# Computing gelu(x U) of three token tiles as dense products and gathering values from a prepared table

## What is computed

```python
def peer(h, w_q, keys, u_tab, v_tab):        # for each block xb of 128 tokens
    q = einsum('td,de->te', xb, w_q).reshape(128, 8, 2, 128)
    s = einsum('thpd,hpkd->thpk', q, keys)                    # scores, two axes of 128 keys
    s_top, i_top = lax.top_k(s, 16)                           # 16 best on each axis
    cand = s_top[:, :, 0, :, None] + s_top[:, :, 1, None, :]  # 256 candidates
    best, sel = lax.top_k(cand, 16)                           # 16 experts a head: eidx
    gate = jax.nn.softmax(best, axis=-1)
    act = jax.nn.gelu(einsum('td,thkd->thk', xb, u_tab[eidx]), approximate=False)
    return einsum('thk,thkd->td', gate * act, v_tab[eidx])
```

## Time and profile before

| | |
|---|---|
| median of 3 runs | 2221.38 us (2214.74 to 2225.39) |
| the profiled execution: span | 2217.6 us |
| busy: TensorE, VectorE, ScalarE, GpSimd | 1812.9, 1313.7, 872.2, 632.8 us |
| moved by DMA | 637 MB, 545 of it by the gathers |
| first gather issued, first dot | 852.6, 859.0 us |
| two ScalarE steps of a slot (L2077, L2082) | 0.20 and 0.29 us |

### The profile page before, as it was taken

The page is one execution under the profiler, slowest core; times in us unless marked ns, Lnnn a source line. Parts: engine busy times, 40 slices in busy tenths (PEclk is TensorE's granted clock), DMA queues, the critical chain, the costliest instruction groups (busy, mean ns, idle before and its releaser), DMA issues.

```text
span 2217.6 us, 25834 instructions
## 1 busy us (share of the span) xinstructions
PE 1812.9 (82%) x8648; PEld 1169.7 (53%) x8648; DVE 1313.7 (59%) x2828; ACT 872.2 (39%) x2271; POOL 632.8 (29%) x553
## 2 busy tenths in 40 slices
PE   5989889979987888898887777777777777777776
PEld 4988889969966887565532222222323322222222
DVE  3127353353363537677766766767667866766764
ACT  4223322242244324444434444444443444444443
POOL 0002012100000002454434444444344443444442
PEclk8999899979998998999999999999999999999999
DMA  3313122335015329999999999999999999999997
GB/s 115 123 44 94 29 58 72 99 104 180 22 65 192 115 76 367 334 413 416 395 393 419 420 419 420 420 420 418 393 420 409 419 418 419 402 420 420 419 415 301
DMA packets 171933, 637.36 MB, mean 287 GB/s; under 512 B 12546, under 2 KB 97605, under 8 KB 104856
## 3 DMA queue, kind: packets, MB, share of 16 engines
q0 software_dynamic: 74880, 545.29, 60.0%
q1 hardware_dynamic: 96928, 90.50, 12.9%
HBM read 617.92 MB, written 17.93 MB: 287 GB/s over the span
## 4 chain that ended last, share of the span: by engine, by line
DMA 31%; PE 13%; DVE 8%; ACT 8%; issue 3%; DVEq 0%; ACTq 0%
DMA ex_uv_row<-in_peer_uv,ex_eidx 31%; PE ps L1995 10%; DVE ex_uv_row L2228 5%; ACT ex_spread L2087 2%; ACT L2077 1%; ACT ret_tables L2082 1%; ACT L2071 1%; PE ps L570 1%; PE ps L572 1%; PE ps L571 1%; ACT ret_tables L2077 1%; DMA ex_uv_row<-in_peer_uv,ex_eidx_s 1%; DVE ex_fin L2236 0%; DVE ex_w_lo L2162 0%; DVE ex_top_i L2190 0%
## 5 line engine op out<-in xcount | busy, mean ns | idle before, releaser
L1995 PE MATMUL ps<-ex_uv_row,ex_spread 128*128 128x512 f32 (+1 forms) x2016 | 964.0, 612 | 278.8 <-ACT ex_spread L2087 278.3
L1954 POOL DMA_INDIRECT ex_uv_row<-in_peer_uv,ex_eidx x512 | 561.2, 1096 | 1004.6 <-PE ps L1995 716.3
L2228 DVE CUSTOM_DVE_ANT_0 ex_uv_row<-ex_uv_row,x_ffn 128x1024 f32<-128x1024 f32 x512 | 624.2, 1225 | 360.4 <-DMA ex_uv_row<-in_peer_uv,ex_eidx 356.1
L1995 PEld LDWEIGHTS ps<-ex_uv_row,ex_spread 128*128 128x128 f32 (+1 forms) x2016 | 351.0, 189 | 851.5 <-issue 851.3
L2077 ACT ACTIVATE ret_tables<-ret_tables 128x1 f32<-128x1 f32 x520 | 104.9, 202 | 644.8 <-DVE ret_tables L2228 643.4
L2087 ACT ACTIVATE ex_spread<-square,ret_tables 128x128 f32<-128x128 f32 (+1 forms) x504 | 201.5, 400 | 16.5
L2082 ACT ACTIVATE ret_tables<-ret_tables 128x1 f32<-128x1 f32 x512 | 150.6, 294 | 17.1 <-ACT ret_tables L2077 0.2
L570 PE MATMUL ps<-proj_b_whi,x_lo 128*128 128x256 f32 (+1 forms) x320 | 91.1, 285 | 7.4 <-DVE proj_b_wlo L479 7.0
L570 PE MATMUL ps<-x_hi,ex_w_lo 128*128 128x260 f32 (+1 forms) x272 | 90.7, 334 | 6.1 <-DVE x_lo L2279 3.1
L572 PE MATMUL ps<-proj_b_whi,x_hi 128*128 128x256 f32 (+1 forms) x320 | 90.6, 283 | 0.0
L571 PE MATMUL ps<-proj_b_wlo,x_hi 128*128 128x256 f32 (+1 forms) x320 | 90.6, 283 | 0.0
(11 more groups left out here) (408 smaller groups left out, 3234.5 us busy)
## 6 DMA issues: line engine op xcount, KB each, us to landing
first_raw<-in_w_in SPq DMA_DIRECT2D x8, 1024.0 KB, 8.6
ex_uv_row<-in_peer_uv,ex_eidx POOLq DMA_INDIRECT x512
dp_w_raw<-in_w_in SPq DMA_DIRECT2D x14, 512.0 KB, 4.1
proj_a_raw<-in_w_in SPq DMA_DIRECT2D x4, 1024.0 KB, 5.2
cv_w_raw<-in_w_in SPq DMA_DIRECT2D x8, 512.0 KB
proj_b_raw<-in_w_in SPq DMA_DIRECT2D x4, 1024.0 KB, 5.4
S_sample<-in_state_ret SPq DMA_DIRECT2D x1, 4096.0 KB, 22.3
out_ret_s<-S_sample SPq DMA_DIRECT2D x4, 1024.0 KB, 4.4
```

The source lines that it names most:

```text
L1954: pool.indirect_dma_start(uv_row[:, p % RING, :], None, a["peer_uv"][0], bass.IndirectOffsetOnAxis(ap=index_of(n), axis=0)).then_inc(row_l ...
L1995: ins = pe.matmul(k.pv[j % 2][0:r, c, :], spread[:, p % RING, 0:r], uv_row[:, p % RING, D + c * 512:D + (c + 1) * 512], start=first, stop= ...
L2228: dve.tensor_tensor_reduce(u, u, x, 1.0, 0.0, ALU.mult, ALU.add, coef[:, n:n + 1]).then_inc(dotted, 1)
```

## The change

U no longer comes by gathers for tiles 1 to 3. The product of all their tokens with the whole of U is formed densely.

- The host lays out U transposed in 128 blocks of 128 experts (`peer_ut`), 512 KB each, 4096 bytes contiguous in each partition. An *activity block* loads one of them, rounds it on ScalarE, splits it on VectorE or GpSimd in turn, multiplies it on TensorE (24 instructions of 384 columns), takes the Gelu on ScalarE (128 x 384) and stores it (1536 bytes for each expert).
- A new table in DRAM, `value_rows`, has a row for each expert: its V row (4096 bytes) and its 384 activities (1536 bytes), 5632 bytes. V is copied into it, DRAM to DRAM, by 16 transfers of 4 MB on ScalarE's queue: four in `convolve` (after SiLU 0, 3, 6 and 9) and twelve in `delta_solve` (after every second copy of Y).
- The order of slots becomes: tile 0 (128), the sample (8), tiles 1, 2, 3 (384). The first 136 keep the gather of joined rows (`gather_pair`), and tile 0's are all added by VectorE. They are worked off beside the 144 blocks (16 query blocks, two before each unit's 16 activity blocks; 128 activity blocks), one slot per activity block, three blocks behind.
- The 384 slots of tiles 1 to 3 gather whole rows of `value_rows` (`gather_value`, 128 x 5632 bytes) into ten buffers in the place of the seven. They wait until all copies and stores are done and the first 136 slots are used. VectorE picks each token's own activity by the diagonal, times the gate (`picked`), in one small instruction; there is no dot and no Gelu. TensorE adds 294 of them, VectorE 90 (one in four).
- The retrieval of a unit now runs two units ahead in the value stage, and in the dense stage at fixed blocks. Weight buffers are three instead of two.

```diff
+    def copy_values(self, act):
+        n = self.copies
+        part = slice(n * NE // COPIES, (n + 1) * NE // COPIES)
+        act.dma_start(self.value_rows[part, 0:D], self.peer_uv[part, D:2 * D]).then_inc(self.values_copied, 16)
+        self.copies = n + 1
@@ convolve, scalar
                     act.activation(pre[:, c, 0:NP_TOK], taps[:, c % 2, :], ACT.Silu).then_inc(silu_done, 1)
+                    if c % 3 == 0:
+                        k.copy_values(act)
@@ delta_solve, scalar
                         act.activation(Y[:, n % 2, :, :], bank(4 + n % 2), ACT.Copy).then_inc(y_done, 1)
+                        if n % 2 == 0:
+                            k.copy_values(act)
@@ experts, sync
+                def load(i):
+                    kind, n = blocks[i]
+                    if i >= DEEP:
+                        lowered(sp, i - DEEP)
+                    src = columns(a["peer_wq"][0], n * P, P) if kind == "q" else a["peer_ut"][n]
+                    sp.dma_start(w_raw[i % DEEP][:, :, :], src).then_inc(w_loaded[i % DEEP], 16)
+                def store(b):
+                    sp.wait_ge(z_made, b + 1)
+                    to = k.value_rows[b * P:(b + 1) * P, :]
+                    sp.dma_start(to[:, D:WROW], z_rows[:, b % DEEP, :]).then_inc(z_stored[b % DEEP], 16)
@@ experts, gpsimd
+                for i, (kind, n) in enumerate(blocks):
+                    if kind == "z" and AHEAD <= n - LAG + AHEAD < PAIRS and n >= LAG:
+                        gather_pair(n - LAG + AHEAD)
+                    if 5 <= i + 2 < len(blocks) and not by_dve(i + 2):
+                        lower(pool, i + 2)
+                for p in range(NE // P - LAG + AHEAD, PAIRS):
+                    gather_pair(p)
+                pool.wait_ge(k.values_copied, 16 * COPIES)
+                pool.wait_ge(vector_done, HK)
+                pool.wait_ge(v_done, PER_ROW)
+                for b in range(DEEP):
+                    pool.wait_ge(z_stored[b], 16 * len(range(b, NE // P, DEEP)))
+                for p in range(PAIRS, SLOTS):
+                    gather_value(p)
@@ experts, tensor
+                def activities(i, b):
+                    lowered(pe, i)
+                    wait(pe, z_made, b - 1)
+                    mm3(pe, k.pb[b % 2][:, 0:BT], DC, lambda x, c: x[:, c, :], w_hi[i % DEEP], w_lo[i % DEEP],
+                        lambda x, c: x[:, c, P:NP_TOK], x_hi, x_lo).then_inc(z_mm, 1)
@@ experts, scalar
+                for i, (kind, n) in enumerate(blocks):
+                    if i and blocks[i - 1][0] == "z":
+                        activate(blocks[i - 1][1])
+                    elif i:
+                        take(blocks[i - 1][1], 0)
+                        take(blocks[i - 1][1], 1)
+                    if i and i + 2 < len(blocks):
+                        upper(i + 2)
+                    if kind == "z" and n >= LAG:
+                        row(n - LAG)
+                    if kind == "z" and n in weight_at:
+                        weight(weight_at[n])
@@ experts, vector
+                for i, (kind, n) in enumerate(blocks):
+                    if kind == "z":
+                        if n >= LAG:
+                            dot(n - LAG)
+                        if n >= LAG + 1:
+                            add_vector(n - LAG - 1)
+                        if n in retrieve_at:
+                            retrieve(*retrieve_at[n])
+                        if n in normalise_at:
+                            normalise(normalise_at[n])
+                    if 5 <= i + 2 < len(blocks) and by_dve(i + 2):
+                        lower(dve, i + 2)
+                def picked(p):
+                    n, m = order[p], p - PAIRS
+                    z = value_slot(p)[2]
+                    dve.wait_ge(gated, place[n // TOPK] + 1)
+                    dve.wait_ge(value_loaded[m % VALUES], 16 * (m // VALUES + 1))
+                    if p in by_vector:
+                        own.fence(dve.tensor_tensor_reduce(z, z, k.eye, gate_of(n), 0.0, ALU.mult, ALU.add, coef[:, n:n + 1]))
+                    else:
+                        wait(dve, v_done, on_tensor[p] - SPREADS + 1)
+                        dve.scalar_tensor_tensor(spread[:, on_tensor[p] % SPREADS, :], z, gate_of(n), k.eye,
+                                                 ALU.mult, ALU.mult).then_inc(diagonal, 1)
```

More of the change, by code:

```diff
@@ L1810, in experts @@
-    add_at = [end + 3 for end in ends[:-1]]
-    by_vector = {*VECTOR_FIRST, *range(HK * TILES - VECTOR_LAST, HK * TILES)} | {TOPK * u + i for u in range(1, PH - FIRST) for i in VECTOR_AT}
-    rows_upto = lambda p, kind: sum((n in by_vector) == kind for n in order[:p])
+    PAIRS = HK + PER_ROW
+    LAST = TILES - 1
+    order = [*range(HK), *range(HK * TILES, SLOTS), *range(HK, HK * TILES)]
+    tiles = [0, TILES, *range(1, TILES)]
+    ends = [p + 1 for p, n in enumerate(order) if p + 1 == SLOTS or order[p + 1] // HK != n // HK]
@@ new lines, in experts @@
+    add_at = {ends[j] + 3: j for j in range(1, NT - 1)}
+    turns = [*range(PH), SAMPLE, *range(PH, UNITS)]
+    place = {x: j for j, x in enumerate(turns)}
+    blocks = expert_blocks()
+    at_z = {n: i for i, (kind, n) in enumerate(blocks) if kind == "z"}
+    rests = {HK + PER_ROW + 4 * m + 3 for m in range((SLOTS - PAIRS) // 4)}
+    late = {PAIRS + m for m in range(12)} | {ends[3] + m for m in range(12)}
+    by_vector = {*range(HK), *(rests - late), *range(SLOTS - VECTOR_LAST, SLOTS)}
+    rows_upto = lambda p, kind: sum((m in by_vector) == kind for m in range(p))
@@ L1835, in experts @@
+        x_of = lambda t: x_first if t == 0 else x_rest[:, t - 1, :]
+        v_rows = flat(uv_row)
         sem = lambda n: k.sem("ex_" + n)
-        pair = lambda n: [k.sem(f"ex_{n}{b}") for b in range(2)]
-        w_loaded = pair("w_loaded")
-        rounded, split, q_mm, q_done = (sem(n) for n in ("rounded", "split", "q_mm", "q_done"))
-        s_mm, s_free, own_s, idx_ready, expd, cleared, gated = (sem(n) for n in
-            ("s_mm", "s_free", "own", "idx_ready", "expd", "cleared", "gated"))
@@ L1841, in experts @@
-        row_loaded = [sem(f"row_loaded{b}") for b in range(RING)]
-        dotted, weighed, spread_done, v_done, vector_done = (sem(n) for n in
-            ("dotted", "weighed", "spread_done", "v_done", "vector_done"))
-        h_loaded = pair("h_loaded")
-        summed, squared, rooted, ready, sample_gate = (sem(n) for n in
-            ("summed", "squared", "rooted", "ready", "sample_gate"))
-        stored = pair("stored")
+        several = lambda n, count: [k.sem(f"ex_{n}{b}") for b in range(count)]
@@ L1936, in _ @@
+                store(blocks[-1][1])
+                for j in range(NT):
                     result(j)
@@ new lines, in _ @@
+                for i in (2, 3, 4):
+                    lower(pool, i)
+                for p in range(AHEAD):
+                    gather_pair(p)
[5 more added lines that the diff above has]
+                for p in range(NE // P - LAG + AHEAD, PAIRS):
+                    gather_pair(p)
@@ L1969, in scores @@
                     wait(pe, s_free, j - 1)
-                    for p in two:
+                    for p in range(2):
                         out = score_bank(j)[0:r, p * NK:(p + 1) * NK]
@@ L2019, in _ @@
                 pe.wait_ge(keys_done, 1)
-                for n in two:
-                    pe.wait_ge(split, n + 1)
+                for n in range(2):
+                    lowered(pe, n)
                     ins = mm3(pe, k.pb[4][:, n * P:(n + 1) * P], DC, lambda x, c: x[:, c, :], w_hi[n], w_lo[n],
@@ L2246, in add @@
                 def add(j):
                     r = ROWS[tiles[j]]
+                    last = ends[j] - (VECTOR_LAST if j == NT - 1 else 0)
+                    wait(dve, vector_done, on_vector[last])
+                    dve.wait_ge(h_loaded[j % 2], 16 * (j // 2 + 1))
+                    if j == 0:
+                        dve.sem_inc(summed, 1)
+                        return
                     dve.wait_ge(v_done, on_tensor[ends[j]])
-                    wait(dve, vector_done, on_vector[ends[j] - (VECTOR_LAST if j == NT - 1 else 0)])
@@ new lines, in _ @@
+                for p in range(NE // P - LAG, PAIRS):
+                    dot(p)
+                    if p <= HK:
+                        add_vector(p - 1)
+                    if p == HK:
+                        add(0)
+                    if p in (HK - 2, HK, HK + 2, HK + 4):
+                        retrieve(PH + 1, (p - HK + 2) // 2)
+                    if p == HK - 1:
+                        normalise(PH)
+                scale(0)
+                normalise(PH + 1)
+                for p in range(PAIRS, SLOTS):
+                    u, i = divmod(order[p], TOPK)
+                    picked(p)
+                    if p - 1 in by_vector and p - 1 >= PAIRS:
+                        add_vector(p - 1)
+                    if i in PARTS_AT and u + 2 < UNITS:
+                        retrieve(u + 2, PARTS_AT.index(i))
```

(2 more changed lines are left out.)

432 lines of the change are left out of this document (241 added, 191 removed).

## The result

Over four runs each, the changed kernel takes 2362.72 us (2354.7 to 2365.87), the kernel before 2218.26: a ratio of 1.0639, 95% interval 1.0607 to 1.0671. The forecast was 2267 with a range from 2195 to 2325. The sign was right, the size was not: 144 us were lost where 46 were forecast.

What follows compares the result with a forecast made beforehand. The prediction took the kernel as bound by its engines up to 830 us, then by DMA. Its sum was 861 + 637 + 33 + 676 + 11.5 = 2218.5, plus 45 for copies = 2264, 2267 as median; range 2195 to 2325.

Steps and rivals of the forecast that it cites:

- The bound: Whole kernel before the change: bound by its engines up to 830 us with DMA idle, by DMA after it.
- The dense stage: Activity and query blocks: seven units of 81 us, the last 70; 637 us, ends 616 and 665; TensorE bound by a hair.
- 4% of stalls: Dense stage: allowance added to the unit's 78.0 us of TensorE because TensorE and DMA are close, giving 81 us.
- Start and drain: Ends of the dense stage: activity blocks from 861 to 1498 us, then 33 us of drain until values arrive from 1531.
- The value stage: The 383 further value gathers at 1.74 us each, 1.5% over the floor: 676 us, ends 659 and 705.
- price line: DMA prices, a line through pieces of 512 and 8192 bytes: 217 ns for 5632 bytes, 1.74 us a value gather.
- The copies: Convolution and delta solve: 16 copies of V delay side loads that ScalarE waits for; 15 and 30 us lost.
- ten periods x 2.4 to 5: Delta solve: loss per period from copies, 2.4 us by bandwidth to 5 by full latency, over ten periods; taken as 30.
- sharing by time: Faster rival: DMA engines share by time, not piece, between queues; copies' 45 us and 21 of the dense stage vanish, 2201; chance 0.20.
- Copies carried over by the queue without loss: No-difference rival, copy stages: stalls only as bandwidth forces, copies carried into later stages; 0 to 15 us, 2222 to 2232; chance 0.12.
- Coupled dense stage: Rival in the dense stage: chain across three in-order queues makes splits late, 88 us a unit, 2316; chance 0.13.
- A gather of 2.0 us: Rival in the value stage: gathers do not speed up as their bytes do, 98 us more, 2365; chance 0.05.

Runs made afterwards that it cites:

- half loads: Changed kernel with each activity block from the ninth on loading only half of its transposed U tile, so activities are wrong; 2357.52 us.
- the wide loads: Changed kernel with side tiles' weights laid out so a load has 128 pieces of 4096 bytes in place of 1024 of 512; 2299.64 us.

## Why the prediction failed, step by step

- **The bound** was read rightly: the value stage runs at a DMA share of 1.02. That the experts' stage gains nothing was forecast too: 1393 us, 1392.1 before, 1408.8 measured.
- **The dense stage**: from its first blocks (about 990.5) to the last activation at 1630.6, 640 us for 637, and 80.6 us a unit for 81. The total was right and its parts were not. Products of 384 columns start 175 ns apart (median from 1100 to 1500 us), not 171; that makes TensorE's unit 79.5 us, not 78, and with 398.6 of 400 us busy it has hardly a stall. The six inner units take 79.2 to 80.6 us, the first 86.3. DMA needs 0.96 of 80, 77, where I had 72.5; but its share is no fixed amount of work, since with half loads the bytes fall by 14% and the share by 6%. VectorE needs 71 (357 of 400), where I had 61, because of GpSimd's splits. That 4% of stalls covered all this was luck.
- **Start and drain** were right: the first blocks begin 37.6 us behind the stage's start, where I had 35.5; from the last activation to the first value used 34.2 us, where I had 33. The tail was 10.5, where I had 11.5.
- **The value stage** took 686 us for 676: 1.79 us a gather at 415 GB/s, where the price line gave 1.74 and 1.5% over it. This is 10 of the 17 us that the experts' stage lost, inside the 659 to 705.
- **The copies** are the step that failed, "Together 45, ends 0 and 80": they cost 127 us, 54 in the convolution (15 forecast) and 73 in the delta solve (30). The mechanism was right, pieces by turns and ScalarE's rounding that holds up Y and with it TensorE; its terms were mis-sized. First, I wrote that a load "lands some 13 us after its issue": behind one copy it is rounded after 18, since its first piece comes 5 us later and a copied piece takes 189 ns and not 161. Second, I counted one copy for each load ("a copy falls into every period of 11.1 us"): a load that is still under way 8.5 us after its issue meets the next copy too, and then is rounded after 23.4. Third, I took "ten periods x 2.4 to 5"; there are twelve copies, and each costs 73 / 12 = 6.1 us, above my upper price. Fourth, in the convolution I added bandwidth ("12 or more: 15"), while the DMA share there is 0.73: it is not full, its loads are late. One copy costs 13.5 us there, since each of the loads that ScalarE already waited for the earlier trace rows now waits for a copy. The upper end of 80 was only twice the middle, with no row that bounded a load behind a DRAM to DRAM copy; the chance of a larger loss was held by two other rivals, both wrong.
- **The rivals**: sharing by time is refuted by the wide loads. Copies carried over by the queue without loss: refuted by the 127 us. Coupled dense stage at 88 us: no, 80.6. A gather of 2.0 us: no, 1.79.

## What to carry to other kernels

"DMA is idle there" is no reason to call a background copy free. Ask which loads are in flight beside it, in how many pieces, and who waits for them: a load of many small pieces pays about one of the copy's pieces for each of its own, and once it is late it meets the next copy too. 16 MB cost 1 us in a stage where nobody waits for such loads (as 16 copies from GpSimd) and over 50 in one where ScalarE does (as 4 copies from its own queue). Lay such loads out in large pieces first, then put the copies where nobody waits for a load. When a sum of near-equal resources comes out right, halve one of them before believing its parts.

## What the runs showed of the hardware

- A DMA of 8192 pieces held its issuing engine for 17 us and moved at 174 GB/s in mean, a DMA of 1024 pieces held it for 0.5 us.
- A load issued 2.4 us behind a copy of 1024 pieces moved its first piece after 6.5 us, with hardly a copied piece in front after 1.3. A load of 1024 pieces of 512 bytes was rounded after 18.1 to 18.6 us behind one copy and 23.4 to 23.9 behind two.
- A piece of 4096 bytes from DRAM to DRAM took 189 ns on the mean beside the loads.
- Products of 384 columns, each with its own load of weights, started 175 ns apart, those of 260 columns 120.
- VectorE's addition of 128x1024 with both operands in the buffer memory took 1802 ns on the mean with GpSimd's splits beside it, 1280 without, and GpSimd's gathers 1439 and 1146.
- A TensorE that waits for its operands also works more slowly: the granted clock was 0.83 from 361 to 432 us where it was 1.00 in the same stage of before.
